# Whole-array transposes of the probabilities, and attention steps cut into two halves of projection work

## What is computed

```python
# layer A, for each block of 128 queries (window 128 to either side, plus 256 context keys)
q, k, v, g = split(u @ w_in)
q, k = apply_axial_rope(q, rope), apply_axial_rope(k, rope)
s = concatenate([where(mask, q @ k_window.T * scale, NEG_INF), q @ k_ctx.T * scale, sink])
p = softmax(s)[..., :-1]
o = p @ concatenate([v_window, v_ctx])
y = (o * silu(g)) @ w_out
# layer B, for each row of the grid: s = q @ k_region.T * scale + bias, masked; s_ctx = q @ k_ctx.T * scale
# p = softmax([s, s_ctx]); o = p_lat @ v_region + p_ctx @ v_ctx; y = (o * silu(g)) @ w_out
```

## Time and profile before

| | |
|---|---|
| Median of 3 runs | 2187.4 us (2183.41 to 2189.2) |
| The profiled execution | 2189.2 us, of which 2186.9 us is the span of the profile |
| TensorE matmul busy | 2040.6 us (93% of the span), 14404 instructions |
| VectorE busy | 1068.7 us (49%), 2164 instructions |
| ScalarE busy | 871.4 us (40%), 1632 instructions |
| GpSimd busy | 826.1 us (38%), 594 instructions |
| DMA | 157.52 MB, mean 72 GB/s |

### The profile page before, as it was taken

One profiled execution on the slowest core, in us unless ns is written; L12 is line 12 of the kernel. 1 busy time (PEld: TensorE's weight loads), 2 busy tenths in 40 slices (PEclk: granted clock), 3 DMA queues, 4 the chain that ended last, 5 costly groups with the idle time before them and its releaser, 6 DMA issues.

```text
span 2186.9 us, 35896 instructions
## 1 busy us (share of the span) xinstructions
PE 2040.6 (93%) x14404; PEld 1700.1 (78%) x14404; DVE 1068.7 (49%) x2164; ACT 871.4 (40%) x1632; POOL 826.1 (38%) x594
## 2 busy tenths in 40 slices
PE   5999999999989899999999699889999999999795
PEld 4888888887878778877777588778888888887684
DVE  4556567558555555445555623623443333334424
ACT  4110100100125465666766600645555555555401
POOL 3333333333346422211221225554434454355266
PEclk9999999999999999999999689999999999999798
DMA  4323322332223200000000223221121111213143
GB/s 167 106 87 97 106 87 77 116 90 73 78 87 112 73 33 21 32 33 33 32 21 23 101 92 111 77 88 49 40 58 48 43 46 49 58 32 104 44 144 111
DMA packets 49475, 157.52 MB, mean 72 GB/s; under 512 B 5408, under 2 KB 8608, under 8 KB 49184
## 3 DMA queue, kind: packets, MB, share of 16 engines
q1 hardware_dynamic: 48304, 153.97, 22.0%
q10 hardware_dynamic: 1008, 1.27, 0.2%
HBM read 134.51 MB, written 20.71 MB: 71 GB/s over the span
## 4 chain that ended last, share of the span: by engine, by line
PE 80%; DVE 9%; issue 4%; ACT 3%; POOL 2%; DMA 1%; SPq 0%; POOLq 0%; DVEq 0%; ACTq 0%
PE psum L765 21%; PE psum L767 20%; PE psum L766 20%; PE psum L919 7%; PE psum L880 6%; PE psum L896 4%; DVE logits L1432 2%; ACT logits L1106 1%; POOL out_tile L742 1%; PE psum L775 1%; DVE win L1228 1%; PE psum L785 1%; DVE prob_t L1449 1%; PE psum L847 1%; DVE u_lo L1466 1%
## 5 line engine op out<-in xcount | busy, mean ns | idle before, releaser
L765 PE MATMUL psum<-u_hi,w_hi 128*128 128x512 f32 (+1 forms) x1440 | 546.8, 380 | 9.0 <-DVE u_lo L1350 5.2
L602 POOL CAST w_hi<-w_raw 128x1024 fp32r<-128x1024 f32 x144 | 160.4, 1114 | 1042.1 <-DMA w_raw<-weights_in 1042.1
L766 PE MATMUL psum<-u_lo,w_hi 128*128 128x512 f32 (+1 forms) x1440 | 529.1, 367 | 0.0
L767 PE MATMUL psum<-u_hi,w_lo 128*128 128x512 f32 (+1 forms) x1440 | 528.7, 367 | 0.0
L604 POOL TENSOR_TENSOR w_lo<-w_raw,w_hi 128x1024 fp32r<-128x1024 f32 x144 | 360.4, 2503 | 11.5
L765 PEld LDWEIGHTS psum<-u_hi,w_hi 128*128 128x128 f32 x1440 | 275.7, 191 | 59.3 <-issue 5.7
L767 PEld LDWEIGHTS psum<-u_hi,w_lo 128*128 128x128 f32 x1440 | 275.4, 191 | 45.3
L766 PEld LDWEIGHTS psum<-u_lo,w_hi 128*128 128x128 f32 x1440 | 276.1, 192 | 39.5
L1106 ACT ACTIVATE logits<-logits,neg_max 128x640 f32<-128x640 f32 (+2 forms) x288 | 225.7, 784 | 53.1 <-DVE neg_max L1432 51.1
L1124 ACT ACTIVATE prob_t<-psum 128x320 f32<-128x320 f32 (+1 forms) x288 | 119.0, 413 | 301.2 <-PE psum L896 301.2
L765 PE MATMUL psum<-x_hi,w_hi 128*128 128x512 f32 x512 | 201.5, 394 | 29.0 <-DVE x_lo L1213 25.2
(11 more groups left out here) (141 smaller groups left out, 3089.4 us busy)
## 6 DMA issues: line engine op xcount, KB each, us to landing
w_raw<-weights_in SPq DMA_DIRECT2D x144, 512.0 KB, 3.6
w_ada<-w_ada_in SPq DMA_DIRECT2D x48, 512.0 KB, 3.6
residual<-act_buf SPq DMA_DIRECT2D x4, 2048.0 KB, 7.3
res<-residual SPq DMA_DIRECT2D x32, 256.0 KB, 3.5
tab<-bias_tab_in SPq DMA_DIRECT2D x16, 496.5 KB
act_buf<-x_t_in SPq DMA_DIRECT2D x8, 512.0 KB, 13.1
out<-out_tile SPq DMA_DIRECT2D x8, 512.0 KB, 2.6
staged<-a_y SPq DMA_DIRECT2D x6, 640.0 KB, 2.9
```

Of the source, the lines that this page charges most:

```text
L602: pool.tensor_copy(w_hi[:, slot, :], w_raw[:, slot, :]).then_inc(w_hi_done, 1)
L765: pe.matmul(out, wh, xh, start=first, stop=False)
L766: pe.matmul(out, wh, xl, start=False, stop=False)
L767: return pe.matmul(out, wl, xh, start=False, stop=last)
```

## The change

The transposes of the probabilities become whole: one transpose of 128 queries by 128 keys where there were two of 64 queries, with the whole identity as the moving operand. Their target is now banks 4 and 5 as one stretch of 640 columns, so a head's transposes wait until those of the head before have been copied out. The copy is one instruction a head of 128 by up to 640, on VectorE for head 0 and on ScalarE for head 1, where each engine had copied one half of both. `ps_out` moves from bank 3 to the end of bank 5: the wait of `outputs` for later logits and the wait of `scores` for `gated` go, a wait of `turn_probs` for `gated` comes, and `outputs` of a step waits for both copies of the following step.

The projection work of a pair is cut into twice as many parts. TensorE's order in a step becomes: scores of `g + 1`, turn head 0 of `g`, a half of work, turn head 1 of `g`, the other half, outputs of `g - 1`. ScalarE and VectorE take the chunks of the two halves at two places, and `rope_times` counts in halves.

```diff
--- before.py
+++ after.py
@@ -180,7 +180,7 @@
 
 
 
-PARTS = tuple([in_parts(row, TILES[layer]) for row in STAGES[layer][1:]] + [[[] for _ in range(TILES[layer])]]
+PARTS = tuple([in_parts(row, 2 * TILES[layer]) for row in STAGES[layer][1:]] + [[[] for _ in range(2 * TILES[layer])]]
               for layer in range(2))
 
 
@@ -190,12 +190,12 @@
 
 def rope_times(pair):
 
-    parts, last = PARTS[0][pair], TILES[0] - 1
+    parts, last = PARTS[0][pair], 2 * TILES[0] - 1
     times = {}
     for n, part in enumerate(parts):
         for c in ended(part):
             if c.kind in "qk" and c.n == 1:
-                times[c.kind, c.pair] = tuple(min(n + d, last) for d in (0, 2, 3))
+                times[c.kind, c.pair] = tuple(min(n + d, last) for d in (1, 4, 5))
     return times
 
 
@@ -351,8 +351,8 @@
 
     pj = [bank(6), bank(7)]
     ps_score = [bank(0, 2), bank(2, 2)]
-    ps_pt = [bank(4), bank(5)]
-    ps_out = bank(3)[:, HALF - P:HALF]
+    ps_pt = bank(4, 2)
+    ps_out = bank(5)[:, HALF - P:HALF]
     ps_rows = [bank(2 * n, 2) for n in range(ROW_SLOTS)]
     ps_back = bank(4, 2)
     c_silu = [bank(2 * who, 2) for who in range(2)]
@@ -383,7 +383,7 @@
     tab_loaded, bias_ready = sem("tab_loaded"), sem("bias_ready")
     score_done, logit_done, prob_done = sem("score_done"), sem("logit_done"), sem("prob_done")
     rec_done, prob_scaled = sem("rec_done"), sem("prob_scaled")
-    pt_done, pt_act, pt_dve = sem("pt_done"), sem("pt_act"), sem("pt_dve")
+    pt_done, pt_free = sem("pt_done"), sem("pt_free")
     pv_done, gate_ready, gated = sem("pv_done"), sem("gate_ready"), sem("gated")
     y_stored, y_loaded = sem("y_stored"), [sem(f"y_loaded{k}") for k in range(STAGED)]
     y_hi_done, y_split = sem("y_hi_done"), sem("y_split")
@@ -875,8 +875,6 @@
                 for c, n, keys in spans:
                     for h in range(2):
                         r = slice(h * HD, (h + 1) * HD)
-                        if m == 0 and h == 1 and c == KEYS - C and g >= 3:
-                            pe.wait_ge(gated, g - 2)
                         mm = pe.matmul(ps_score[h][:, P + c:P + c + n], q[r, t * P:(t + 1) * P], keys(k[r, :]),
                                        start=m == 0, stop=m == 2)
                         if m == 2 and c == KEYS - C:
@@ -887,25 +885,21 @@
             s += h
             pe.wait_ge(prob_scaled, s + 1)
             if s:
-                pe.wait_ge(pt_act, s)
-                pe.wait_ge(pt_dve, s)
+                pe.wait_ge(pt_free, s)
+            if h == 0 and g >= 2:
+                pe.wait_ge(gated, g - 1)
             c0 = first_key(layer, t)
             for c in range(key_tiles(layer, t)):
-                for n in range(2):
-                    r = slice(n * HD, (n + 1) * HD)
-                    tr = pe.transpose(ps_pt[n][:, c * HD:(c + 1) * HD], logits[s % SLOTS][r, c0 + c * P:c0 + (c + 1) * P],
-                                      ident[r, r])
+                tr = pe.transpose(ps_pt[:, c * P:(c + 1) * P], logits[s % SLOTS][:, c0 + c * P:c0 + (c + 1) * P], ident[:, :])
             tr.then_inc(pt_done, 1)
 
-        def outputs(layer, g):
+        def outputs(layer, g, last):
 
 
             pair, t, s = steps_of(layer, g)
-            pe.wait_ge(pt_act, s + 2)
-            pe.wait_ge(pt_dve, s + 2)
+            pe.wait_ge(pt_free, s + 2 if last else s + 4)
             if g:
                 pe.wait_ge(gated, g)
-            pe.wait_ge(logit_done, min(s + 6, STEP0[layer] + 2 * PAIRS * TILES[layer]))
             if t == 0 and (layer == 1 or pair % 4 == 0):
                 for c in CHUNKS[layer]["t", pair // 4 if layer == 0 else pair]:
                     consumed(pe, c)
@@ -949,11 +943,12 @@
                 if g + 1 < end:
                     scores(layer, g + 1)
                 turn_probs(layer, g, 0)
-                work(layer, PARTS[layer][pair][t])
+                work(layer, PARTS[layer][pair][2 * t])
+                turn_probs(layer, g, 1)
+                work(layer, PARTS[layer][pair][2 * t + 1])
                 if g > first:
-                    outputs(layer, g - 1)
-                turn_probs(layer, g, 1)
-            outputs(layer, end - 1)
+                    outputs(layer, g - 1, False)
+            outputs(layer, end - 1, True)
 
         def output_projection(layer):
 
@@ -1114,15 +1109,15 @@
             n, pr = s % SLOTS, logits[s % SLOTS][:, first_key(layer, t):KEYS]
             act.activation(pr, pr, ACT.Copy, scale=row_rec[:, n:n + 1]).then_inc(prob_scaled, 1)
 
-        def take_probs(layer, g, h):
+        def take_probs(layer, g):
 
             pair, t, s = steps_of(layer, g)
             n = key_tiles(layer, t)
-            act.wait_ge(pt_done, s + h + 1)
+            act.wait_ge(pt_done, s + 2)
             if g >= 2:
                 act.wait_ge(pv_done, g - 1)
-            act.activation(prob_t[:, g % 2, h, 0:n, 0:HD], ps_pt[0][:, 0:n * HD].rearrange("p (t q) -> p t q", q=HD),
-                           ACT.Copy).then_inc(pt_act, 1)
+            act.activation(prob_t[:, g % 2, 1, 0:n, :], ps_pt[:, 0:n * P].rearrange("p (t q) -> p t q", q=P),
+                           ACT.Copy).then_inc(pt_free, 1)
 
         def start(layer):
 
@@ -1148,18 +1143,18 @@
             for g in range(first, end):
                 pair, t, _ = steps_of(layer, g)
                 more = g + 1 < end
-                if g > first:
-                    take_probs(layer, g - 1, 1)
-                take_probs(layer, g, 0)
                 if more:
                     probs(layer, g + 1, 0)
+                for c in ended(PARTS[layer][pair][2 * t]):
+                    take(layer, c)
+                take_probs(layer, g)
+                if more:
                     probs(layer, g + 1, 1)
                     divide(layer, g + 1, 0)
-                for c in ended(PARTS[layer][pair][t]):
+                for c in ended(PARTS[layer][pair][2 * t + 1]):
                     take(layer, c)
                 if more:
                     divide(layer, g + 1, 1)
-            take_probs(layer, end - 1, 1)
 
         def split_last(layer):
 
@@ -1439,14 +1434,14 @@
             n = s % SLOTS
             dve.reciprocal(row_rec[:, n:n + 1], row_sum[:, n:n + 1]).then_inc(rec_done, 1)
 
-        def take_probs(layer, g, h):
+        def take_probs(layer, g):
 
             pair, t, s = steps_of(layer, g)
             n = key_tiles(layer, t)
-            dve.wait_ge(pt_done, s + h + 1)
+            dve.wait_ge(pt_done, s + 1)
             if g >= 2:
                 dve.wait_ge(pv_done, g - 1)
-            dve.tensor_copy(prob_t[:, g % 2, h, 0:n, HD:P], ps_pt[1][:, 0:n * HD].rearrange("p (t q) -> p t q", q=HD)).then_inc(pt_dve, 1)
+            dve.tensor_copy(prob_t[:, g % 2, 0, 0:n, :], ps_pt[:, 0:n * P].rearrange("p (t q) -> p t q", q=P)).then_inc(pt_free, 1)
 
         def gate_output(layer, g):
 
@@ -1497,24 +1492,23 @@
             for g in range(first, end):
                 pair, t, _ = steps_of(layer, g)
                 more = g + 1 < end
-                if g > first:
-                    take_probs(layer, g - 1, 1)
                 if more:
                     logit(layer, g + 1, 0)
-                take_probs(layer, g, 0)
+                take_probs(layer, g)
                 if more:
                     logit(layer, g + 1, 1)
                     invert(g + 1, 0)
-                    invert(g + 1, 1)
-                for c in ended(PARTS[layer][pair][t]):
-                    take(layer, c)
-                if layer == 0:
-                    rope_due(pair, t)
+                for n in (2 * t, 2 * t + 1):
+                    for c in ended(PARTS[layer][pair][n]):
+                        take(layer, c)
+                    if layer == 0:
+                        rope_due(pair, n)
+                    if more and n % 2 == 0:
+                        invert(g + 1, 1)
                 if g > first:
                     gate_output(layer, g - 1)
                 if pair == PAIRS - 1 and 1 <= t < KT:
                     low_y(layer, t - 1)
-            take_probs(layer, end - 1, 1)
             gate_output(layer, end - 1)
             for n in range(len(y_spans(layer))):
                 low_y(layer, KT - 1, n)
```

## The result

The changed kernel takes 2219.6 us (median of 4 runs, 2215.51 to 2221.58) against 2186.9 of the kernel before (4 runs, 2183.41 to 2189.2): ratio 1.0148, 95% interval 1.0129 to 1.0169: slower by 1.5%. The forecast had the direction; its 2256 us was 36 too high, with a growth of 69 us where 32.7 was measured.

A forecast was written before the change was run, and what follows sets the result against it. TensorE's own work bounds layer B; layer A has some 25 us of waiting, and other engines pace its last pair. 2189.2 + 51 - 9 + 0 + 11 + 15 = 2257, or 2256 us against the median; range 2206 to 2292.

The forecast's parts named there:

- The transposes' price: TensorE in both layers: whole transposes add 0.44 us in each of 115 five-key-tile steps, +51 us, bounds 38 and 68.
- The step's +0.43 us: TensorE, one five-key-tile step: whole transposes, mode change and second beginning of work cost 1.20 us against 0.77 removed.
- the 26 us: Layer A's part of the +51 us for transposes: 59 five-tile steps in seven pairs, at 0.44 us each.
- The scaling by key tiles: Layer A: steps with five, four and two key tiles counted as 42/5 = 8.4 five-tile steps a pair, 59 in seven.
- I price the new stalls like the old: 0: Layer A's change of pair: new waits behind ScalarE's queue cost as much as the old; 0 us, bounds -8 and +7.
- The gate's waits: Layer A: the scores' waits for the gated output shrink, with some of the transposes' 12.6 us; -9 us, bounds 0 and -20.
- The named wait: Layer A: TensorE's 9.7 us in front of the scores, for the gated output, expected to shrink to 2 to 3.
- The value chunks in B: Layer B's pair ends: second value chunk waits 1.6 us for ScalarE's copy of the last gate chunk; +11 us, bounds 0 and +14.
- The last pairs: Both layers' last pairs, without projection work as cover: a longer chain per step; +15 us, bounds 0 and +30.
- The ring: Last pairs: chain from logit to logit of the same head, 6.74 us before, 7.6 us and engine hops after.
- rival (b): Faster: a whole transpose costs 0.062 us, A's stalls go, last pairs shorten; 2158 to 2170 us, chance 0.07.
- Rival (a): Transposes cost TensorE less than thought and removed waits are real: 2198 us at the bounds, middle 2224; chance 0.22.

The follow-up runs named there:

- the pair of kernels with neither wait: Kernel before and changed kernel, both without the gates' Silu and with rotary work cut to 32 columns: 2146.9 us (ratio 0.9831) and 2195.7 us (1.0064).
- the run with the old layer B: Changed kernel's layer A with the gate product ahead of the rotary sum, layer B as in the kernel before: 2181.7 us against 2183.7, ratio 0.9991.

## Why the forecast was wrong

**The transposes' price: right in B, too high in A.** The step's +0.43 us was measured as 0.39, and whole transposes followed each other at about 0.1 us, as in the earlier trace rows. 56 steps make 22 of the 27.6 us. In A the 26 us was about 16: an argument from the pair of kernels with neither wait (9.9 us of time and 5.9 of waits that went). The scaling by key tiles overcharged steps with two.

**The step that failed: the stall at the change of pair, "I price the new stalls like the old: 0".** It was worth -14 us (21.2 without the Silu before, 7.3 after). The mechanism was read rightly, that the copy for which the next turn waits stood behind the Silu and no longer does. What I put against it was mis-sized: the division and the next copy are late, but behind half a part of work the waits are 0.28 and 0.66 us at three changes and nothing at three; only the change to the last pair costs 3.7. And the old stall was larger than its row: 3.0 us a pair, of which I had counted the 1.94 us of one row. Of the other 9.6 us of the seven pairs, 1.6 lie around the waits themselves (3.29 us for 1.09, a row of 1.94), 4 are projection work at half clock behind three of them, and the rest is spread. Two kernels with the same waits have three and five such falls, so the -14 is uncertain by some 3 us.

**The gate's waits: -9 forecast, about -7 measured, partly by luck.** Layer A's -5.2, less the +16 and the -14, leaves -7. The named wait fell from 9.7 to 5.7, not to 2 or 3, and of the rotary work's cost only 2 us was won (8.4 to 6.3). The other waits that went, in the pair of kernels with neither, are mostly the outputs' for the logits, 4.0 us around the change to the last pair, which the forecast had counted with the last pairs.

**The value chunks in B: right cause, +11 became +5.** The wait came where it was forecast, at 0.98 us; TensorE was at the second value chunk 2.1 us after the turn (forecast 1.8), ScalarE ready after 3.0 (forecast 3.4). The earlier trace rows held only half of the old waits there, but the other half stayed nearly as it was (2.0 to 2.7).

**The last pairs: +15 became +6.** The ring is as I drew it, VectorE's copy, turn, ScalarE's copy, outputs, but I put the outputs of every step at the halved clock of the earlier trace rows. The granted clock rose to 0.80 and 0.74 in these windows, where the same stretches of the kernel before had 0.67 and 0.66. In A's last pair the rings whose outputs took 2.40 us are 7.4 to 8.3 us long (before 6.4 to 6.7), as forecast; those whose outputs ran at full clock, in 1.31, are 6.2 and 6.3. One of the latter (1225.55 to 1231.88):

```profile
1225.55 0.88 DVE L1427 CUSTOM_DVE_ANT_0 logits<-psum,a_mask,sink_neg 128x640 f32<-128x640 f32 x1
...
1228.85 1.31 PE L913 MATMUL psum<-prob_t,a_v 128*64 128x128 f32 x20 [0.79 <-ACT prob_t L1119]
...
1231.88 0.88 DVE L1427 CUSTOM_DVE_ANT_0 logits<-psum,a_mask,sink_neg 128x640 f32<-128x640 f32 x1
```

Of the two kernels with one part of the change each, that with whole transposes in the old order had 0.89 and 0.85 in these windows, that with halves in the new order 0.71 and 0.68, so the clock seems to go with the whole transposes. But these are single profiles, and kernels with the same code in a window differ there by up to 0.16. That TensorE's longer work in each step is the reason fits and isn't shown.

**Missing from the sum:** 3.4 us between the layers. Of these, 1.2 lie in B's first two steps: from the first value transpose to the first product with values it is 19.8 us before, 21.0 after, and 19.8 again in the run with the old layer B. Another 1.4 lie in a spell of half clock some 135 us behind A's end (1395.3 to 1398.7), which the profile of the kernel before doesn't have. It stands in that of the kernel before without the Silu (216.7 us between the layers, where the other kernels with the old order have 213 to 214) and in that with the old layer B (217.4) too, so it doesn't come from B's order. Why it comes is open.

In numbers: 68 forecast against the profiled execution, less 13 for the transposes (51 to 38), 14 for the Silu, 9 for the last pairs and 6 for the value chunks, plus 2 for the gate's waits and 3.4 between the layers: 31. The stages from A's first product to B's last differ by 31.8 in the two profiles, the medians by 32.7.

Two slips in the forecast's own working: rival (b) names gains of 20 and 22 us but takes off 36, where they make 42 and its lower end 2152; and the range begins at 2206, which is 8 us above the 2198 that it is said to round.

Rival (a), the transposes dear but A's waits gone, was the nearest, at 2224 us; I gave it 0.22. Of rival (b) nothing came true: no whole transpose was near 0.062 us.

## What to carry to other kernels

A part of a change can be right only in the order it was made for: count the changes between half-array and whole-array instructions that an order makes in each step before moving either. A stall can cost more than the row that shows it: here a row of 1.94 us cost 3.0, in part because the granted clock fell at three of these waits. Leaving out the instruction that causes it, in both kernels, prices it in one run each. And where engines run fixed queues, taking a wait out of one place mostly shows who stood behind it: here four of six attempts to move an instruction earlier or later made the kernel slower.

## What the runs showed of the hardware

- Costs are from start to start of the bursts. Five whole float32 transposes of 128 by 128 cost 0.46 us between pieces of whole-array work, 0.52 after scores on half arrays, and 0.70 between products with values and scores. The same five as ten halves cost 0.33 between outputs and scores, 0.39 to 0.44 between scores and work, and 0.46 between pieces of work. The neighbours are worth up to 0.24 us a burst of whole ones.
- The first 512-column product behind transposes cost 0.31 (whole) or 0.34 us (halves), the last one in front of half-array instructions 0.32, those between 0.23.
- Two half-array transposes side by side cost 0.067 us and a whole one about 0.1: packing won a factor of about 1.5.
- At three of the five waits of 1.94 us between pairs with work TensorE's granted clock fell from 1.00 to 0.50, and 512-column products followed each other at 0.43 us instead of 0.23; at the other two it stayed.
- A table load of ScalarE took 1.28 us, and the Silu started 1.30 us after the load did.
